# The edges of an expert stage: norms, router, last norm and bias table rewritten in a one-core transformer kernel

## The reference, cut to what matters

```python
x = x + gt_m * rmsnorm(merged @ w_out, g_mix_post)
h2 = rmsnorm(x, g_ffn_pre) * (1 + sc_f) + sh_f
logits = h2 @ w_router + b_router                # 256 tokens x 32 experts
top_logit, top_e = lax.top_k(logits, 4)          # the lower index wins a tie
top_w = softmax(top_logit)
# each expert, on the tokens that chose it:
a = clamped_swiglu(xb @ w_gate[e] + b_gate[e], xb @ w_lin[e] + b_lin[e])
y = a @ w_down[e] + b_down[e]                    # weighted, added up to ffn
x = x + gt_f * rmsnorm(ffn, g_ffn_post)
```

## Time and profile before

| | |
|---|---|
| median of 3 runs | 2760.7 us (2759.15 to 2763.48) |
| the profiled execution's own time | 2759.07 us |
| its span in the trace | 2757.4 us |
| TensorE busy | 2506.6 us (91%) |
| VectorE busy | 1225.0 us (44%) |
| ScalarE busy | 859.1 us (31%) |
| GpSimd busy | 43.4 us (2%) |
| read from HBM | 683.70 MB, 249 GB/s over the span |
| expert stage and last norm | from 1732.15 us to the end |

### The profile page before, as it was taken

How to read it: one execution, slowest core, us unless ns; L and a number is a source line. 1 busy time by engine, 2 the same in 40 slices (tenths; PEclk the granted TensorE clock), 3 DMA queues, 4 the chain that set the end, 5 groups by cost and what they waited for, 6 DMA issues and landing times. The chain is left out here.

```text
span 2757.4 us, 34161 instructions
## 1 busy us (share of the span) xinstructions
PE 2506.6 (91%) x12924; PEld 1674.1 (61%) x12925; DVE 1225.0 (44%) x1958; ACT 859.1 (31%) x1384; POOL 43.4 (2%) x61
## 2 busy tenths in 40 slices
PE   3998999899799899989989999499999999999997
PEld 2887989688588798868867789333333333333332
DVE  2754665565475476556554464522221211211212
ACT  2444444444444454444443443111010000100101
POOL 0000000000000000000000001100000000000000
PEclk9999999999899999999999999699999999999999
DMA  5763433575375344357552124499999999999984
GB/s 222 256 209 115 151 131 117 198 263 186 143 258 206 111 148 133 121 207 251 190 146 77 56 91 130 187 421 428 429 429 428 429 428 428 429 429 428 429 340 195
DMA packets 113182, 687.46 MB, mean 249 GB/s; under 512 B 20642, under 2 KB 21922, under 8 KB 87362
## 3 DMA queue, kind: packets, MB, share of 16 engines
q1 hardware_dynamic: 105140, 651.41, 61.1%
q0 software_dynamic: 7488, 29.36, 3.0%
q10 hardware_dynamic: 432, 5.08, 0.4%
HBM read 683.70 MB, written 2.11 MB: 249 GB/s over the span
## 5 line engine op out<-in xcount | busy, mean ns | idle before, releaser
L2149 PE MATMUL ps<-wexp_all_second,con_all_whole 128*64 128x512 f32 x3168 | 705.3, 595 | 28.7 <-DMA wexp_all_second<-in_w_lin 28.6
L2149 PEld LDWEIGHTS ps<-wexp_all_second,con_all_whole 128*64 128x64 f32 x3168 | 220.5, 137 | 468.9 <-issue 395.7
L446 DVE TENSOR_TENSOR lo_first<-raw_first,hi_first 128x1024 fp32r<-128x1024 f32 x264 | 308.5, 1220 | 42.0 <-ACT hi_first L416 42.0
L241 PE MATMUL ps<-hi_first,h_hi_first 128*128 128x512 f32 x704 | 285.8, 406 | 22.1 <-DVE lo_first L446 22.1
L242 PE MATMUL ps<-lo_first,h_hi_first 128*128 128x512 f32 x704 | 280.0, 398 | 0.0
L243 PE MATMUL ps<-hi_first,h_lo_first 128*128 128x512 f32 x704 | 279.7, 397 | 0.0
L416 ACT CAST hi_first<-raw_first 128x1024 fp32r<-128x1024 f32 x264 | 260.6, 1055 | 20.6 <-DMA raw_first<-in_ffn_wgu 20.6
L241 PE MATMUL ps<-h_hi_first,w_hi_first 128*128 128x256 f32 x848 | 247.4, 292 | 3.2 <-DVE w_lo_first L891 3.2
L242 PE MATMUL ps<-h_lo_first,w_hi_first 128*128 128x256 f32 x848 | 238.5, 281 | 0.0
L243 PE MATMUL ps<-h_hi_first,w_lo_first 128*128 128x256 f32 x848 | 238.2, 281 | 0.0
L891 DVE TENSOR_TENSOR w_lo_first<-raw_first,w_hi_first 128x1024 fp32r<-128x1024 f32 x122 | 148.6, 1222 | 158.2 <-ACT w_hi_first L802 157.6
(11 more groups left out here) (430 smaller groups left out, 3387.1 us busy)
## 6 DMA issues: line engine op xcount, KB each, us to landing
wexp_all_second<-in_w_gate SPq DMA_DIRECT2D x64, 2048.0 KB, 23.0
wexp_all_second<-in_w_lin SPq DMA_DIRECT2D x64, 2048.0 KB, 25.6
wexp_all_second<-in_w_down SPq DMA_DIRECT2D x64, 2048.0 KB, 20.4
raw_first<-in_ffn_wgu SPq DMA_DIRECT2D x176, 512.0 KB, 4.9
raw_first<-in_w_mix SPq DMA_DIRECT2D x138, 512.0 KB, 3.4
raw_first<-in_ffn_wd SPq DMA_DIRECT2D x88, 512.0 KB, 5.2
raw_second<-in_w_mix SPq DMA_DIRECT2D x57, 512.0 KB, 3.3
wada_first<-in_w_ada POOLq DMA_DIRECT2D x48, 512.0 KB, 5.1
```

The source lines that it names most:

```text
L241: nc.tensor.matmul(out, w_hi, x_hi, start=start, stop=False, skip_group_check=True)
L446: nc.vector.tensor_tensor(lo[:, slot], raw[:, slot], hi[:, slot].bitcast(F32), ALU.subtract).then_inc(s[f"{kind}_lo"], 1)
L2149: mm = nc.tensor.matmul(dst[side(half), :], lhs(k), B.wexp[2 * "gld".index(kind) + part][:, k % 4, half * HALF:(half + 1) * HALF], start=( ...
```

## The change

1. **Bias table.** Its four loads move on SyncE's queue from the end to just behind the first of the eight chunks of `w_out`. The five operations move from GpSimd to VectorE, one behind each of five `lower` steps. GpSimd has no work left in the mixer.
2. **Table preload.** ScalarE takes a square root of an unused number at the end of the mixer, and another behind the expert loop.
3. **Norms.** The multiplication by the gain row now comes ahead of the norm factor, as an operation of its own, so that it needs no statistics; the norm factor and the following addition are one operation.
4. **Router.** Both tiles run one behind the other through turn, copy, product and selection, with a bank and a semaphore count each. The comparison of all pairs is replaced: `max` finds the eight largest logits, the last four of them are overwritten with a very low number, `match_replace` marks the places of the other four, and a comparison makes `sel`.
5. **SyncE's wait** before its loop is for `ends`, and not for the whole list.
6. **Last norm** in the expert stage: no phase boundary in front of it.

```diff
+def bias_part_dve(dve, nc, s, B, n):
+    part = (n + 1) // 2
+    rest = slice(0, (3 - part) * E)
+    if n == 0:
+        dve.wait_ge(s["b_in"], 64)
+    else:
+        dve.wait_ge(s["b_part"], n)
+    if n % 2:
+        nc.vector.tensor_tensor(B.braw[rest], B.braw[rest], B.btri[rest], ALU.subtract).then_inc(s["b_part"], 1)
+    else:
+        nc.vector.tensor_copy(B.btri[rest], B.braw[rest]).then_inc(s["b_part"], 1)
...
             for c in range(1, N_MIX2):
                 load(c)
+                if c == N_MERGE2:
+                    sp.wait_ge(s["near_ready"], TC)
+                    sp.wait_ge(s["decay_out"], 2)
+                    sp.wait_ge(s["prod"], 1)
+                    bias_table_sp(sp, s, B, I)
...
+            nc.scalar.activation(B.stats[:, 2, 3:4], B.stats[:, 1, 3:4], ACT.Sqrt).then_inc(s["std_ready"], 1)
+            act.wait_ge(s["std_ready"], 3)
...
             for c in range(N_MERGE2 + SPLIT - 1, N_MIX2):
                 lower(c)
+                if c - (N_MERGE2 + SPLIT - 1) < 5:
+                    bias_part_dve(dve, nc, s, B, c - (N_MERGE2 + SPLIT - 1))
...
-            sp.wait_ge(s["listed"], 1)
+            sp.wait_ge(s["ends_ready"], 1)
...
         def _(pe):
-            pe.wait_ge(s["htok_ready"], TC)
-            turn_pe(nc, s, B, B.htok, x_bank)
-            pe.wait_ge(s["h2_copied"], 4)
             for t in range(TC):
+                pe.wait_ge(s["htok_ready"], t + 1)
                 for k in range(KD):
+                    mm = nc.tensor.transpose(h_bank(t, k // 4)[:, (k % 4) * P:(k % 4 + 1) * P], B.htok[:, t, k * P:(k + 1) * P],
+                                             con("ident"))
+                    if k % 4 == 3:
+                        mm.then_inc(s["x_turned"], 1)
+                for k in range(KD):
+                    if k % 4 == 0:
+                        pe.wait_ge(s["h2_copied"], 2 * t + k // 4 + 1)
+                    mm = nc.tensor.matmul(ps[:, t, 0:E], B.h2[:, k, t * P:(t + 1) * P], B.w_r[:, k, :], start=(k == 0), stop=(k == KD - 1))
+                mm.then_inc(s["logits"], 1)
...
+            for n, t in enumerate((1, 0)):
+                if n:
+                    dve.wait_ge(s["squared"], 1)
+                tt(B.acc[:, t, :], mixed[t], B.rows[:, 0, :], ALU.mult)
             rstd_dve(dve, nc, s, B, slice(0, TC), TC)
             for t in range(TC):
-                stt(B.acc[:, t, :], mixed[t], B.stats[:, 3, t:t + 1], B.rows[:, 0, :], ALU.mult, ALU.mult).then_inc(s["tmp_ready"], 1)
-                dve.wait_ge(s["tmp_ready"], t + 1)
-                tt(B.x[:, t, :], B.x[:, t, :], B.acc[:, t, :], ALU.add).then_inc(s["x_ready"], 1)
+                stt(B.x[:, t, :], B.acc[:, t, :], B.stats[:, 3, t:t + 1], B.x[:, t, :], ALU.mult, ALU.add).then_inc(s["x_ready"], 1)
...
-            for t in range(TC):
-                other, this = bcast(B.lg[:, t, :], 1, E), bcast(B.lg[:, t, :], 2, E)
-                ch.link(tt(B.cmp, other, this, ALU.is_equal))
-                ch.link(tt(B.cmp, B.cmp, con("earlier"), ALU.mult))
-                ch.link(tt(B.cmp2, other, this, ALU.is_gt))
-                ch.link(tt(B.cmp, B.cmp, B.cmp2, ALU.add))
-                ch.link(red(B.sel[:, t, :], B.cmp, AX, ALU.add))
+            for t in range(TC):
+                dve.wait_ge(s["logits"], t + 1)
+                ch.link(tt(B.lg[:, t, :], ps[:, t, 0:E], B.v2("b_router"), ALU.add))
+                ch.link(nc.vector.max(B.top[:, t, :], B.lg[:, t, :]))
+                ts(B.rmax[:, t:t + 1], B.top[:, t, 0:1], -1.0, None, ALU.mult).then_inc(s["max_ready"], 1)
+                ch.link(nc.vector.memset(B.top[:, t, TOPK:], ABSENT))
+                ch.link(nc.vector.match_replace(B.chosen[:, t, :], B.top[:, t, :], B.lgx[:, t, :], CHOSEN))
+                tt(B.sel[:, t, :], B.chosen[:, t, 0:E], B.lg[:, t, :], ALU.is_gt).then_inc(s["sel_ready"], 1)
...
+            for t in range(TC):
+                dve.wait_ge(s[f"added{t}"], total + 1)
+                tt(B.htok[:, t, :], B.acc[:, t, :], B.rows[:, 3, :], ALU.mult).then_inc(s["y_gained"], 1)
+            rstd_dve(dve, nc, s, B, slice(0, TC), 3 * TC, 3)
+            for t in range(TC):
+                stt(B.x[:, t, :], B.htok[:, t, :], B.stats[:, 3, t:t + 1], B.x[:, t, :], ALU.mult, ALU.add).then_inc(s["x_done"], 1)
```

119 lines of the change are left out of this document (47 added, 72 removed).

## The result

The changed kernel takes 2734.9 us in the median of 4 runs (2727.35 to 2738.98), beside 2762.1 for the kernel before: a ratio of 0.990, with a 95% interval of 0.9875 to 0.9924. It is faster by 1.0%, where 2734 was predicted. Its profiled execution has a time of 2732.81 us and a span of 2731.1, that is 26.3 less span than before.

A forecast was written before the change was run, and what follows sets the result against it. The expert stage was taken as a weight stream at 428 GB/s with slow head and tail. Gains 2.1 + 7.0 + 0.8 + 11.8 = 21.7 at the head and 4.8 at the tail, 26.5, gave 2734 us, range 2729 to 2741.

The forecast's parts named there:

- What bounds the kernel: Expert stage: a weight stream at 428 GB/s; moving expert 1's first down issue moves the end by the same amount.
- Only the tail arrives: Rival: weight stream unbroken from the stage's start hides the head's gain, leaving only 4.8 us, 2755.9; chance 0.05.
- signs of being wrong: Down issue moving less than first expert product, TensorE waiting for VectorE late in mixer, or half clock beyond first gate product.
- The stage starts earlier: Mixer's end: without GpSimd's bias table the expert stage starts 2.1 us sooner, bounds 0 and 2.2.
- The norms: Stage's head: first transpose 8.95 us behind the stage's start instead of 15.94; gain 7.0 us, bounds 5.5 to 7.5.
- Turn and product, router: Stage's head: gain 0.8 us in turn and product, 11.8 in the router, the latter with bounds 9.9 to 11.9.
- the slower rival: Router: `max` and `match_replace` cost far more than assumed; gain gone at 7.9 us each, 2766 at 9.2; chance 0.02.
- SyncE's wait: Head of SyncE's loop: gate and linear loads start some 3.6 us earlier, but the queue only runs dry sooner; gain nothing.
- The clock: TensorE's granted clock in the stage's head and first block: same place in the work, so no change counted.
- a rival of 0.15 against: TensorE's clock returns later relative to the shifted work: 1.5 to 3.5 us lost, or 7 us; chance 0.15.
- The tail: Last addition to last result: 10.5 us becomes 5.65; gain 4.8 us, bounds 4.3 to 5.1.

The follow-up runs named there:

- u4_router: Changed kernel with the router's comparison of all pairs again, per tile in the new pipeline: median 2742.41 us, ratio 0.9932, stage 1009.64.
- w2_short: Changed kernel with 10 unused 128x512 products ahead of TensorE's first wait in the stage: median 2731.41 us, ratio 0.9897, stage 997.73.
- w3_fill: Changed kernel with 10 unused products at the stage's start and five more in TensorE's pauses: median 2728.19 us, ratio 0.9888, stage 992.67.
- after: The changed kernel itself, in its first profile, against the kernel before: median 2734.9 us, ratio 0.990, stage 1002.84.
- u2_pool: Changed kernel with the bias table on GpSimd and its loads at the queue's end, as before: one run, 2736.77 us, stage 1000.66.
- u2_again: Changed kernel with the bias table on GpSimd and its loads at the queue's end, now timed: median 2737.59 us, ratio 0.9906, stage 1000.78.
- p_late: Changed kernel with the bias table on GpSimd, loads at the queue's end, and one GpSimd cast done twice: one run, 2733.63 us, stage 1000.88.
- u6_norms: Changed kernel with both norms of the stage's head in their old form, preload and order by tiles kept: one run, 2741.59 us, stage 1006.28.
- u3_tables: Changed kernel without both square-root table preloads: one run, 2736.98 us, stage 1001.95.
- u1_list: Changed kernel with SyncE waiting for the whole list again: median 2735.21 us, ratio 0.9901, stage 1002.79.
- same: The changed kernel run again without any edit: median 2734.93 us, ratio 0.9899, stage 1002.73.
- u5_lastnorm: Changed kernel with the last norm in a phase of its own and in its old form: one run, 2738.52 us, stage 1007.18.

## Why the prediction was right, and where only its sum was

**What bounds the kernel.** Right in the main, and confirmed twice: a shift of the first down issue arrived whole at the end (21.59 and 21.64), and in u4_router, w2_short and w3_fill the stage's length moved from after's by +6.8, -5.1 and -10.2 where the down issue moved by +6.9, -5.0 and -10.3. "Only the tail arrives" is refuted by the same numbers. One of the prediction's own signs of being wrong did come true: the down issue moved by less than the first expert product, 21.59 against 23.21. The difference is the clock's, below; the stream behind it did what was said.

**The stage starts earlier.** 2.36 for 2.1. The price of the bias table beside `lower` was hidden as argued (31.31 us against 31.27); the operations took 1.21 and 2.27 us, 8.2 together, and not 12.3, since a cast to bfloat16 of 2048 elements costs what a pass of 1024 does. What the prediction missed is a hazard that the change removes: GpSimd beside VectorE. In the profiled execution of the kernel before it cost TensorE nothing: the last `lower` step began 0.49 us ahead of GpSimd's subtraction and took 1.49, held only by the tail of the cast ahead of it. In both executions of u2_pool's kernel it began 0.11 us behind the subtraction, and the mixer ended 4.5 us later (2.60 of waiting and 1.9 of half clock). The 2.60 us of the earlier trace rows, for which the prediction gave no mechanism, was the same thing: the step ended 1.08 behind the end of GpSimd's cast. The Trainium skill (SBUF — State Buffer, "Who interferes with whom") says that such a pair shares a port under an exclusive lock and that the order of issue decides who blocks; the rows of u2_again and p_late agree, with an end 1.10 and 1.09 us behind GpSimd's.

**The norms.** 6.98 for 7.0, and its parts were measured: 3.45 for the new form (u6_norms), 1.0 for the table (u3_tables); the remaining 2.5 is put down to the second tile's two passes (1745.50 to 1748.04 before), for which the first transpose no longer waits; no run took that alone away.

**Turn and product, router.** 0.97 and 12.0 for 0.8 and 11.8. `max` took 0.20 and the replacement 0.27, where 0.25 each was chosen out of 0.19 to 1.22; pricing them by the rows of the same width was the right choice, and the slower rival, which needed 7.9 us, was far off. The Trainium skill's rule (VectorE: DVE Perf Modes, "Two Vector instructions with no wait between them") is borne out: the replacement is two instructions. The first, MATCH_VALUE_LOAD, costs 0.09 us, where the prediction took 0.2 for it.

**SyncE's wait.** Nothing, as said (u1_list). The gate issue at 1766.25 instead of about 1765 is the slow gate product.

**The clock.** This term, put at nothing with a rival of 0.15 against, is where the forecast was wrong: -0.63 and -1.62, together 2.25. The rival described what happened, a gate product partly at half speed and no fall later, and its 1.5 to 3.5 us hold the 2.25. That the total came out all the same was luck. 1.53 us of the 26.3 arose ahead of the mixer's last product and aren't the change's: at the `lower` step ahead of the first bias part the two traces already stood 1.57 us apart (1697.35 and 1695.78). Gains of 0.2 to 0.4 over the forecast in four terms made up for the rest. Without the 1.53 the change gave 24.7 us in this pair of executions. The medians differ by 27.2 and 27.8, but with intervals of some 21 to 35 and 24 to 32 us, so they can't tell 24.7 from 26.5.

What sets the return is open in part, but it isn't drawn anew in each execution. The stage has the same head in after, same, u1_list and u5_lastnorm. In all four the clock fell 2.7 to 2.9 us behind the stage's first issue and returned 36.8 to 37.0 behind it, though that issue itself stood anywhere from 1728.26 to 1734.91; the two executions of u2_pool's kernel both had it at +29.1. The microsecond of the return in same (from +36) and in u2_again (from +29), as windows:

```profile
1767.77:1768.77 1.00, 1.00 (x4) 0.23 (x2) 0.86 (x5) 0.00 (x0) 0.00 (x0) 0.58 0.00 0
```

```profile
1765.32:1766.32 1.00, 0.75 (x4) 0.56 (x4) 0.93 (x4) 0.16 (x2) 0.00 (x0) 0.94 1.15 492
```

Two places occur: 1.7 to 2.6 us ahead of the first gate product (before, u2_pool, u2_again, p_late, u3_tables), or 5.1 to 5.6 us into it (after, same, u1_list, u4_router, u5_lastnorm, u6_norms; the runs with added products are left aside). Moving the work or moving the fall was enough to change the place. In u3_tables the clock fell at +2.8, as in after, but the gather stood 1.0 us later. In u2_again and p_late the gather stood at +24.8, as in after, but the clock fell at +1.8 and 1.9 us ahead of the stage. The Trainium skill (TensorE: Matmul & The Clock Gate, "What's actually happening") has a monitor that runs free of the program, and the prediction took from it that the return is a matter of chance. The rows agree that it matters how the work lies against the changes of level, but not that this is a new draw in each execution; why it repeats to 0.2 us wasn't tried. A return ahead of the gate product makes the stage 1000.7 to 1000.9, one inside it 1002.7 to 1002.8: 2 us, inside the prediction's "1.5 to 3.5".

**The tail.** 5.2 for 4.8: the gain products and the last two passes overlap a little more than was counted. The squares, boundary and passes carry it; the load's 1.28, which the working counted among the gains, would cost only 0.17 in the new form (u3_tables). Missed: 0.54 us between the last result and the end (4.06 in the big phase; 3.52 and 3.47 in a phase of its own). The traces show part of it: GpSimd's clearing of the phase's semaphores takes 0.29 us instead of 0.09, and the stores' last packet ends 0.12 us later, where the second store's packets now follow the first's without a gap. No run took these apart.

## What to carry to other kernels

Find the first load with which a stream becomes unbroken, and price each edit by how far it moves that issue; all else at the head is hidden. Where a short chain of VectorE and ScalarE work leaves TensorE idle, look at the granted clock of what follows: a few unused wide products in the pauses, ended before the first real one, made the stage of the profiled execution 10 us shorter here, two fifths of the 24.7 that the whole change gave, and the median about 5; too many cost 3. Don't put GpSimd work like this beside VectorE operations that TensorE waits for, even when GpSimd seems to have time. And look where a gain arose before crediting it to the change: 1.53 us of this one were there before the changed code ran.

## What the runs showed of the hardware

- **The clock stayed at half beside a busy TensorE.** After, TensorE was busy 23.55 of the 34 us from 1731 on, with a granted clock of 0.50 in the mean. With 10 products of 128x512 ahead of the same work (w2_short) it stood at 1.00 and 0.97 over the first 17 us.
- **The changes of the clock repeated between executions**: the fall to 0.2 us and the return to 0.2 us in four executions with the same head, whose stages began up to 6.7 us apart; 1.0 us of shift in the work moved the return by 6.9 us (u3_tables).
- **A float32 product of 128x512 with a 128x128 weight took 0.87 us**, in two instructions of 0.44 at the full clock, twice what I had put.
- **These GpSimd and VectorE operations block each other until their end**: 1.23 became 5.06 us for VectorE, with 0.11 us deciding it, and 1.88 became 2.77 for GpSimd (p_late).
- **A table load took 1.28 us and was hidden for as long as ScalarE waited anyway**: 1.0 lost in the head, 0.17 in the tail.
